# A hybrid decoder step: attention, retention, pages and sample states between the weight products of the input projection

## The chip, the cores and the metric

One core of a Trainium2 chip runs one inference step of a small hybrid decoder in a single launch. The metric is the device time of that launch in microseconds (us); smaller is better. The engines are TensorE (PE: matrix products, with PEld its weight loads), VectorE (DVE), ScalarE (ACT), GpSimd (POOL, which here only issues DMAs and clears a few tiles) and SyncE (SP, which here issues the DMAs of the weights).

## What is computed

264 tokens (256 of a prompt, and one token for each of 8 samples) go through two layers. The change touches the first mixer, which the reference states so (cut):

```python
proj = x @ w_in                       # 2048 -> 7168 + 2048 columns
qa, ka, va, qr, kr, vr, gr = split(proj)
ya = stick_breaking(qa, concat(past_k, ka), concat(past_v, va))   # 8 heads of 128
    # z = q k^T * scale + bias; log_fail = -softplus(z) where masked
    # w = exp(log_sigmoid(z) + suffix_sum(log_fail)); y = w v
qr, kr = rotary(qr), rotary(kr) * scale
yr, s_new = retention(qr, kr, vr, s0)                             # 8 heads, value width 256
    # s_new = gamma**n * s0 + k^T v (decayed); y = (q k^T * decay) v + q s0 (decayed)
yr = rms(yr) * silu(gr)
out = concat(ya, yr) @ w_out
```

For the prompt there is no past and the states start at zero. Each sample has 256 past positions in 2 pages of 128 (keys and values: 32 pages of 512 KB in all) and a retention state of 8 x 128 x 256 (half of it is 512 KB; 16 halves, each read, renewed and written back).

## The kernel before, in words

Activations lie feature-major: a tile of 128 features by 264 tokens (`T`) is a matmul's moving operand, and a weight block of 128 x 128 its stationary one. Each of the float32 weights is split into a high and a low part (`hi`, `lo`, in the format fp32r that the products use), as are the activations (`xh`, `xl`), and three matmuls (hi x xh, hi x xl, lo x xh) make one product. The weights come as chunks of 1 MB (128 x 2048): SP loads a chunk into one of the slots of `raw`, ScalarE writes `hi` (`split_hi`), VectorE writes `lo` over `raw` (`split_lo`), both two chunks ahead, and TensorE works through the chunk in four steps of 12 matmuls, one for each accumulator `acc0` to `acc3`. I call such a quarter of a chunk a step. Four chunks make a panel of 512 output columns, which ScalarE or VectorE then evicts.

The phases of weight products stand in a list (`plan`): ab (the input projection above, 72 chunks), out_ab (24), up0, down0, bc, dt, ssd (64), out_ssd, up1, down1. `products` has a hook, `side(j, n)`, which is called behind step n of chunk j and may issue other matmuls; ssd already runs its whole mixer that way: per group of 8 heads (8 groups) it issues 8 spreads (L2045), 8 state reads (L2055), 8 head products (L2076, L2077), a state product of 8 matmuls (L2084, L2085), transposes (L1786) and a few more, all between the products of 64 chunks.

The first mixer does not. Before, ab runs as a loop of 9 turns of two panels without a side. Then TensorE does stick-breaking attention, rotary turns and page scores in one block of code, page values and retention in a second, the samples' states in a third (`ret_outer`, `ret_read`), and the normalization of the heads in a fourth, before the first product of out_ab. There a page or a state is the stationary operand and one column the moving one:

```python
m = mm(aux[3][:, c:c + 1], pg[:, h, :], pt[:, QA + h, SEQ + b:SEQ + b + 1], ...)   # page_scores
```

Pages pass through 3 buffers (`page`), states through 5 (`s0buf`), loaded and stored by POOL in the order of its program, which also holds the waits for the buffers. All of these live in the space of `xh`, `xl` and `x`, which the projection no longer needs then. The gates (silu of `gr`) go to DRAM and back.

Of the kernel before, what the change touches and what calls it, by code (L numbers as in the profile page):

```python
# [7 lines left out]
F32 = mybir.dt.float32  # L8
# [7 lines left out]
P = 128  # L16
D = 2048
SEQ = 256
NB = 8
# [37 lines left out]
def raw_slot(j, body):  # L57

    return {1: (0,), 8: (0, 1, 2, 3, 0, 1, 4, 5)}.get(body, range(NRAW))[j] if body in (1, 8) else \
        (j + 1) % (NRAW - 1) if body == 64 else j % NRAW  # L60


def hi_slot(j, body, turn=0):

    return 0 if body == 1 else (j + 1) % (NHI - 1) if body == 64 else (j + turn) % NHI
# [32 lines left out]
def plan():  # L98
    phases = [
        Phase("ab", 9, 2, 4, False), Phase("out_ab", 2, 2, 6, True),  # L100
# [40 lines left out]
YT_AT, HS_AT, BT_AT, CB_AT, ST_AT, XT_AT, LAST_YT = 4, 8, 12, 20, 22, (24, 26), 24  # L141

# [60 lines left out]
def constants():  # L203
# [20 lines left out]
    by_sample = (j[:, None] < 64) & (j[:, None] % 32 == np.arange(NB)[None, :])  # L224
# [23 lines left out]
def param_layout():  # L248
    at = 0
    for name, width in (("lng", 4 * KT), ("lnb", 4 * KT), ("sbias", H), ("fcw", DEPTH * 3 * 2 * FT),  # L250
                        ("fcb", DEPTH * 2 * FT), ("scw", 4 * CT), ("scb", CT), ("dskip", XST),
                        ("normw", XST), ("dtb", 1), ("alog", 1)):
        PARAM[name] = (at, at + width)
        at += width
    return at
# [12 lines left out]
    "att_in", "consts_in", "conv_base", "conv_done", "conv_silu", "conv_tap",  # L268
    "decay_in", "ffn_out", "ffn_state_in", "ffn_sum", "ffn_tile",
    "gate_in", "gate_out", "kv_out", "ln_a", "ln_cen",  # L270
    "ln_delta", "ln_delta2", "ln_fin", "ln_mean", "ln_norm", "ln_qsum", "ln_sq", "ln_sqrt", "ln_sum", "ln_total", "ln_var", "page_in0", "page_in1",
    "page_in2", "page_used", "pages_in", "rn_a", "rn_b", "rn_bc", "rn_inv", "rn_sq", "rn_sqrt", "rn_sum",
    "rot_c", "rot_done", "rot_m", "rot_p", "rs_in0", "rs_in1", "rs_in2", "rs_in3", "rs_in4", "rs_km", "rs_new",
    "rs_o", "rs_out0", "rs_out1", "rs_out2", "rs_out3", "rs_out4", "rs_t", "rs_tc", "rs_y", "rs_yc", "rt_k",
    "rt_out", "rt_p", "rt_s", "rt_st", "rt_stc", "rt_t", "rt_v", "rt_y", "rt_yc", "sb_L",
    "sb_arg", "sb_cap", "sb_e", "sb_incl", "sb_lf", "sb_m", "sb_na", "sb_part", "sb_vs", "sb_vt", "sb_w",
    "sb_y", "sb_ycopy", "sbz", "sbz_s", "sconv_in", "sconv_out", "small_set",
    "ssd_sum", "x_back", "x_hi", "x_in", "x_lo", "x_out", "y_out",
    "dt_raw", "dt_a", "dt_c", "cum_out", "cd_out", "cd_in", "sel_in", "sel_r", "decay_in0", "decay_in1",
# [7 lines left out]
def build(nc, d):  # L287
# [8 lines left out]
    with ctx:  # L296

        NRB = 5
# [3 lines left out]
        with nc.sbuf_tensor("work", [P, 3 * KT * T], F32) as work:  # L302
            pass
        with nc.sbuf_tensor("workr", [P, 3 * KT * T], F32R) as workr:
            pass
# [11 lines left out]
        extra = sb("extra", [P, 3 * 512 + 384 + NB])  # L317
# [42 lines left out]
        banks = [aux, acc]  # L360


        at = 0
        upper, at = carve(work, at, P)
        rot, at = carve(work, at, P)
        mask, at = carve(work, at, 384)
        cap, at = carve(work, at, 384)
        trig, at = carve(work, at, 4, T)
        decay, at = carve(work, at, H, 384)
        tend, at = carve(work, at, H, 2)  # L370
        c0, c1 = CONST["upper"][0], CONST["tend"][1]
        assert at == c1 - c0, (at, c1 - c0)
        work_consts = work[:, 0:at]
        att0 = at
        temps = []
        for _ in range(2):
            zs, at = carve(work, at, 384)
            e_, at = carve(work, at, 384)
            lf, at = carve(work, at, 384)
            temps.append((zs, e_, lf))  # L380
        vtok = []
        ktw = []
        for _ in range(2):
            v, at = carve(work, at, 2, 256)
            vtok.append(v)
            v, at = carve(work, at, 2, P)
            ktw.append(v)
        NPB = 3
        pg0 = at
        page = []  # L390
        for _ in range(NPB):
            v, at = carve(work, at, H, P)
            page.append(v)

        ebuf = [temps[0][1], temps[1][1], carve(stage[:, :, :].rearrange("p a b -> p (a b)"), 0, 384)[0]]
        turned = []
        for _ in range(2):
            v, at = carve(work, at, T)
            turned.append(v)
        retp, _ = carve(pj, KA * T, H, 256)  # L400
        assert at <= 3 * KT * T, (at, 3 * KT * T)

        at = att0
        s0buf = []
        for _ in range(NRB):
            v, at = carve(work, at, H // 2, 256)
            s0buf.append(v)
        vts, at = carve(work, at, 2048)
        assert at <= 3 * KT * T
        kts, _ = carve(work, c1 - c0 - H * 2 - H * 384, 1024)  # L410
        ktm = [carve(work, c1 - c0 - H * 2 - H * 384 + 1024 * (1 + n), 1024)[0] for n in range(2)]

        silg = pt[:, KA:KA + 2 * H, :]
        rinv, at = carve(work, (KT + CK * LOOK) * T, T)
        rsq, at = carve(work, at, 2, 2, T)
        assert at <= 2 * KT * T, at
# [15 lines left out]
        raw_end, hi_end = raw[:, NRAW - 1, :], hi_plain[:, NHI - 1, :]  # L432
# [46 lines left out]
        def obank(h):  # L479

            return acc[h // 2][:, (h % 2) * 256:(h % 2) * 256 + 256]

# [18 lines left out]
        def load_chunk(eng, ph, i, j):  # L501
# [4 lines left out]
            if ph.name == "out_ssd" and i.reg is None and raw_slot(j, ph.body) == NRAW - 1:  # L506
                eng.wait_ge(used, ph.chunk0)
# [47 lines left out]
        def split_loop(eng, ph, split, src, evac, first=0, end=None, led=0, follow=None, mid=None, front=None):  # L555
# [26 lines left out]
            if front is not None:  # L582
                body(Step(0), False, front)
                with eng.Fori(0, stop - 1) as r:
                    body(Step(1, r), False)
# [70 lines left out]
        def _(pool):  # L656
# [7 lines left out]
            for n in range(4):  # L664
                pool.wait_ge(drained, 4 * (PHASES["ab"].panel0 + 14 + n) + 8)
                pool.dma_start(d["gate"][:, 4 * n:4 * n + 4, :], stage[:, :, :]).then_inc(R["gate_out"], 16)


            pool.wait_ge(used, PHASES["out_ab"].chunk0)
            pool.wait_ge(R["x_lo"], XB)  # L670
            c2 = CONST["decay"][0]
            pool.dma_start(work_consts[:, 0:c2 - c0], d["const"][:, c0:c2]).then_inc(R["att_in"], 16)
            pool.wait_ge(drained, 4 * PHASES["out_ab"].panel0 + 4)
            pool.wait_ge(R["pages_in"], 16)
            n = 0
            for cache in ("ck", "cv"):
                for b in range(NB):
                    for k in range(NPG):
                        v = pool.value_load(pages_sb[0:1, b * NPG + k:b * NPG + k + 1], min_val=0, max_val=NPHYS - 1)
                        if n >= NPB:  # L680
                            pool.wait_ge(R["page_used"], n - NPB + 1)
# [28 lines left out]
            for u in range(NRB - 1):  # L710
                ret_load(u)
# [1588 lines left out]
```

## Time and profile before

| | us |
|---|---|
| median of 3 runs | 3424.61 (3418.01 to 3427.3) |
| the profiled execution, own time | 3422.77 |
| its span, first to last instruction | 3421.1 |
| TensorE busy in the span | 3295.0 (96%) |
| VectorE busy | 1980.3 (58%) |
| ScalarE busy | 1638.3 (48%) |
| HBM traffic over the span | 175 GB/s |

TensorE is busy nearly throughout, so the share alone says little. Its clock has two levels, 1.2 and 2.4 GHz; the profile gives the granted mean of a stretch as a part of 2.4 GHz. In the answers by stretch the columns are: the stretch in us from the span's start, its length, the busy time (and number of instructions) of PE, PEld, DVE, ACT and POOL, the granted clock, the share of the 16 DMA engines, GB/s. A matmul on plain float32 shows as two instructions (x2 for one call), one on fp32r as one; "128\*64 128x256" means a stationary operand of 128 x 64 and a moving one of 128 x 256.

### The profile page before, as it was taken

Reading aid. Unit: us, or ns where it says so; the run is one execution under the profiler, and the core shown is the slowest. Engines: PE = TensorE matmul, PEld = TensorE weight load, DVE = VectorE, ACT = ScalarE, POOL = GpSimd, SP = SyncE. Lnnn points to the kernel's source line nnn. Section 1 sums busy time; section 2 is a strip of 40 time slices with the busy share of each in tenths; the row PEclk is TensorE's granted clock in tenths of the full one; section 3 lists DMA queues with packets and bytes.
Section 4 is the critical chain, followed back from the end, with each engine's and each line's share of the span. In section 5 each row is a group of like instructions: output and inputs, shape, how many; then the busy total and the mean of one; then the engine's idle time right before and its main releaser. Section 6 shows DMA issues by size and latency. Waiting matters only on the chain.

```text
span 3421.1 us, 60330 instructions
## 1 busy us (share of the span) xinstructions
PE 3295.0 (96%) x24851; PEld 3123.8 (91%) x24851; DVE 1980.3 (58%) x2487; ACT 1638.3 (48%) x1722; POOL 115.7 (3%) x206
## 2 busy tenths in 40 slices
PE   7999989989899999999899999999998999999997
PEld 7999988769899999999899777777998999999997
DVE  4333332246765565665766666666667565666666
ACT  3333333024554555544456555665645455455453
POOL 0000011100000000000000110110000000000000
PEclk9999968569999999999999999999999999999998
DMA  5444553525344544644455555554543544546452
GB/s 218 174 184 183 192 209 113 181 95 182 132 160 183 196 161 183 211 167 176 151 190 210 188 200 183 194 192 175 195 164 140 196 166 179 195 167 211 166 186 91
DMA packets 93949, 601.94 MB, mean 176 GB/s; under 512 B 10848, under 2 KB 10848, under 8 KB 32128
## 3 DMA queue, kind: packets, MB, share of 16 engines
q1 hardware_dynamic: 68256, 498.17, 38.9%
q0 software_dynamic: 25568, 102.01, 9.0%
q8 instruction: 89, 1.46, 0.2%
q14 instruction: 36, 0.29, 0.0%
HBM read 560.82 MB, written 39.32 MB: 175 GB/s over the span
## 4 chain that ended last, share of the span: by engine, by line
PE 91%; DVE 5%; issue 2%; ACT 1%; DMA 1%; POOL 0%; DVEq 0%; ACTq 0%; POOLq 0%; SPq 0%
PE acc L618 27%; PE acc L619 26%; PE acc L620 25%; PE aux L2055 2%; PE acc L1939 2%; PE aux L1952 2%; PE aux L1846 1%; PE aux L2076 1%; DVE lo L552 1%; PE acc L1857 1%; PE aux L2045 1%; DVE x L1492 1%; PE aux L1786 1%; DVE xl L1498 1%; PE acc L1798 0%
## 5 line engine op out<-in xcount | busy, mean ns | idle before, releaser
L618 PE MATMUL acc<-xh,hi 128*128 128x264 f32 x7552 | 2178.3, 288 | 73.2 <-DVE lo L552 38.0
L619 PE MATMUL acc<-xl,hi 128*128 128x264 f32 x7552 | 2152.8, 285 | 0.0
L620 PE MATMUL acc<-xh,lo 128*128 128x264 f32 x7552 | 2144.5, 284 | 0.0
L618 PEld LDWEIGHTS acc<-xh,hi 128*128 128x128 f32 x7552 | 1428.7, 189 | 122.8 <-issue 69.3
L552 DVE TENSOR_TENSOR lo<-raw,hi 128x2048 fp32r<-128x2048 f32 x473 | 1075.7, 2287 | 625.2 <-ACT hi L542 625.2
L619 PEld LDWEIGHTS acc<-xl,hi 128*128 128x128 f32 x7552 | 1429.4, 189 | 0.7
L620 PEld LDWEIGHTS acc<-xh,lo 128*128 128x128 f32 x7552 | 1426.4, 189 | 0.0
L542 ACT ACTIVATE hi<-raw 128x2048 fp32r<-128x2048 f32 x473 | 894.9, 1907 | 625.7 <-DMA raw<-in_w 370.8
L541 ACT ACTIVATE xh<-pj 128x1056 fp32r<-128x1056 f32 x144 | 156.0, 1084 | 363.6 <-PE acc L620 279.4
L549 DVE TENSOR_TENSOR xl<-pj,xh 128x1056 fp32r<-128x1056 f32 x144 | 180.6, 1254 | 242.7 <-ACT hi L542 239.6
L1310 DVE SCALAR_TENSOR_TENSOR stage<-acc,par,stage 128x255 f32<-128x255 f32 x352 | 168.6, 479 | 24.9 <-DVE stage L1310 24.4
L848 ACT ACTIVATE stage<-acc,par 128x264 f32<-128x264 f32 x176 | 100.4, 570 | 140.9 <-PE acc L620 140.9
L1641 DVE SCALAR_TENSOR_TENSOR x<-aux,pj,x 128x512 f32<-128x512 f32 x64 | 47.9, 748 | 62.5 <-PE aux L2045 62.5
L1443 DVE SCALAR_TENSOR_TENSOR work<-work,acc 128x256 f32<-128x256 f32 x64 | 24.1, 417 | 80.4 <-PE acc L1939 80.4
L2055 PE MATMUL aux<-x,raw 128*8 128x512 f32 x128 | 65.6, 594 | 0.0
L1952 PEld LDWEIGHTS aux<-pj,work 128*128 128x128 f32 x256 | 55.7, 330 | 9.8 <-issue 9.8
L1939 PE MATMUL acc<-work 8*128 8x256 f32 x128 | 60.0, 647 | 3.9 <-DVE work L1432 3.9
L953 ACT ACTIVATE work<-pj 128x528 f32<-128x528 f32 x8 | 5.0, 641 | 120.9 <-DVE pj L1447 116.3
L1952 PE MATMUL aux<-pj,work 128*128 128x1 f32 x256 | 57.0, 353 | 0.0
L1527 DVE TENSOR_TENSOR pj<-stage 128x528 f32 (+1 forms) x44 | 31.2, 708 | 40.5 <-ACT stage L1022 40.5
L1939 PEld LDWEIGHTS acc<-work 8*128 8x128 f32 x128 | 39.9, 325 | 13.7 <-issue 4.2
L1649 DVE SCALAR_TENSOR_TENSOR pj<-pj,par,aux 128x256 f32<-128x256 f32 x32 | 15.3, 480 | 57.9 <-PE aux L2077 57.9
(300 smaller groups left out, 1858.7 us busy)
## 6 DMA issues: line engine op xcount, KB each, us to landing
raw<-in_w SPq DMA_DIRECT2D x473, 1024.0 KB, 4.8
x<-in_ssm POOLq DMA_DIRECT2D x32, 512.0 KB, 3.9
out_ssms<-x POOLq DMA_DIRECT2D x32, 512.0 KB, 3.6
work<-in_ck POOLq DMA_DIRECT2D x16, 512.0 KB, 3.8
work<-in_cv POOLq DMA_DIRECT2D x16, 512.0 KB, 3.8
work<-in_ret POOLq DMA_DIRECT2D x16, 512.0 KB, 4.8
out_rets<-work POOLq DMA_DIRECT2D x16, 512.0 KB, 5.3
pj<-cumd POOLq DMA_DIRECT2D x32, 256.0 KB, 4.2
```

The costliest lines, as they stand in the source:

```text
L541: act.activation(xh[:, CK * s:CK * s + CK, :], src[:, CK * kc:CK * kc + CK, :], ACT.Copy)
L542: act.activation(hi[:, ph.hi(j), :], raw[:, r, :], ACT.Copy).then_inc(hi_done, 1)
L549: dve.tensor_tensor(xl[:, CK * s:CK * s + CK, :], src[:, CK * kc:CK * kc + CK, :], xh[:, CK * s:CK * s + CK, :].bitcast(F32), ALU.subtract)
L552: dve.tensor_tensor(lo[:, r, :], raw[:, r, :], hi[:, ph.hi(j), :].bitcast(F32), ALU.subtract).then_inc(lo_done, 1)
L618: pe.matmul(out, hi[:, s, w], xh[:, a, :], start=kc == 0 and k == 0, stop=False)
L619: pe.matmul(out, hi[:, s, w], xl[:, a, :], start=False, stop=False)
L620: m = pe.matmul(out, lo[:, r, w], xh[:, a, :], start=False, stop=kc == ph.kc - 1 and k == CK - 1)
L848: a(dst(q, n), acc[n][:, 0:T], ACT.Identity, bias=col(bias), scale=col(w))\
L1310: ins = stt(y[:, k:SEQ], h[:, 0:SEQ - k], one(w[:, width - 1 - k, :], n), y[:, k:SEQ], ALU.mult, ALU.add)
L1939: m = mm(obank(h), ktm[b % 2][0:NB, h * P:h * P + P], vts[0:NB, h * 256:h * 256 + 256], start=True, stop=True)
L1952: m = mm(aux[2][:, c:c + 1], s0buf[u % NRB][:, k, e * P:e * P + P], pt[:, QR + h, SEQ + b:SEQ + b + 1], start=True, stop=True)
L2055: mm(bank_ys[0:NB, :], cz[:, NB * b:NB * b + NB], hbuf[u % 3][:, (b % 2) * 512:(b % 2) * 512 + 512], start=b == 0, stop=b == NB - 1).then_ ...
```

## The change

ab becomes one turn of 18 panels, unrolled, with `ab_side` as its side: every matmul of the mixer is issued behind a fixed step s = 4 j + n of the 288 steps. The panels' order changes so that what the mixer needs comes first (a table: `AB_PANELS`, queries and keys of retention first, gates last), and tables of numbers say at which step each piece stands. Pages and states become the moving operand: the stationary one is a block of 128 x 32 in which one column is the query (`zq`, `qd`) or the weight (`wz`) of a head and the others are zero, so that the 8 (or 4) heads accumulate in rows 32 b to 32 b + 31 of one bank. The outer products for the states take stacked high and low parts in fp32r (`kstk`, `vstk`, 72 rows) in place of 8 rows of float32. All of it shares four banks: `outer`, `reads`, `att`, `heads`; `att` is passed from use to use by two counters (`att_full`, `att_free`). The buffers: ab now uses 5 of 6 `raw` slots and 3 of 4 `hi` slots, and the mixer works in the others, in `x_` and in `extra`; states and pages share one ring of 3 slots of 512 KB (before 5 and 3). The norm's square root and reciprocal become Ln and Exp on ScalarE; the gates no longer pass through DRAM; the samples' sticks are summed by a scan on VectorE.

```diff
-        Phase("ab", 9, 2, 4, False), Phase("out_ab", 2, 2, 6, True),
+        Phase("ab", 1, 18, 4, False), Phase("out_ab", 2, 2, 6, True),
...
+AB_PANELS = [("qr", 0), ("kr", 0), ("vr", 0), ("vr", 1), ("qr", 1), ("kr", 1), ("vr", 2), ("vr", 3), ("qa", 0),
...
+RET_AT = [56 + 16 * h for h in range(H)]
+UNIT_AT = [(78, 142)[u // NB] + 5 * (u % NB) for u in range(2 * NB)]
+SB_AT = [200 + 9 * h for h in range(H)]
+KPAGE_AT = [190 + 2 * n for n in range(NB * NPG)]
+VPAGE_AT = [240 + 2 * n for n in range(NB * NPG)]
+RET_OUT, SB_OUT, PAGE_TURN, PAGE_BACK = 13, 11, 234, 275
...
+            for n in range(3):
+                ring_load(n)
...
+                pool.wait_ge(R["rs_new"], 4 * (n + 1))
+                pool.dma_start(ret_half(d["rets"], n), unit[n % 3]).then_inc(R[f"ring_out{n % 3}"], 16)
...
+            for n in range(units + 2, units + 2 * NB * NPG):
+                ring_load(n)
+                if n == units + NB * NPG + 4:
+                    pool.wait_ge(drained, 4 * AB_PANELS.index(("va", 1)) + 8)
+                    pool.dma_start(d["kv"], pt[:, KA:KA + 2 * H, :]).then_inc(R["kv_out"], 16)
...
-            products(pe, PHASES["ab"], 0)
...
+            def outer_of(u, x):
+
+                pe.wait_ge(R["rs_km"], u + 1)
+                pe.wait_ge(R["att_free"], ATT["vs", 2 * (u // NB) + x] + 1)
+                if u or x:
+                    pe.wait_ge(R["rs_new"], 4 * u + 2 * x)
+                for k in range(2 * x, 2 * x + 2):
+                    m = mm(outer[:, (k % 2) * 256:(k % 2) * 256 + 256], ktm[u % 2][0:72, k * P:k * P + P],
+                           vstk[0:72, k * 256:k * 256 + 256], start=True, stop=True)
+                m.then_inc(R["ob_full"], 1)
+
+            def read_unit(u, x):
+
+                b = u % NB
+                pe.wait_ge(R["qd_set"], u + 1)
+                pe.wait_ge(R["rs_new"], 4 * u + 2 * x + 2)
...
+                for k in range(2 * x, 2 * x + 2):
+                    m = mm(reads[32 * (b % 4):32 * (b % 4) + 32, o:o + 256], qd[u % 2][:, k, :], unit[u % 3][:, k, :],
+                           start=k == 0, stop=k == 3)
...
+            def page_scores(n, x):
 
                 b, k = n // NPG, n % NPG
                 pg = page_at(n)
...
+                for h in range(4 * x, 4 * x + 4):
+                    m = mm(reads[32 * (b % 4):32 * (b % 4) + 32, o:o + P], zq[b % 2][:, h, :], pg[:, h, :],
+                           start=h == 0, stop=h == H - 1)
...
+            products(pe, PHASES["ab"], 0, ab_side)
```

Three places in the order of the program. First TensorE in the attention and the page scores. Before (aux and acc are the PSUM banks, pj the projected tiles, work the buffers), outside of any product:

```order
L1805 MATMUL acc<-pj 128x256
L1806 MATMUL acc<-pj 128x128
L1798 MATMUL acc<-pj,work 128x264
L1846 MATMUL aux<-pj,work 128x1 x8
L1786 MATMUL aux<-cons,pj 128x128 x2
L1822 MATMUL aux<-work 128x384
L1823 MATMUL aux<-work,cons 128x128
L1846 MATMUL aux<-pj,work 128x1 x8
```

Now, at steps 200 and 201 (L625 to L627 are the weight products, x holds the page):

```order
L627 MATMUL acc<-xh,lo 128x264
L2143 MATMUL aux<-pj 128x256
L2144 MATMUL aux<-pj 128x128
L2185 MATMUL aux<-x 32x128 x4
L625 MATMUL acc<-xh,hi 128x264
L626 MATMUL acc<-xl,hi 128x264
L627 MATMUL acc<-xh,lo 128x264
```

The page scores of one page were 8 matmuls of one moving column; they are now two calls of four matmuls of 128 moving columns, behind two consecutive steps, and a head's scores (L2143, L2144) stand in front of one of them.

Second TensorE in the samples' states. Before, 16 units in a row (L1939 the outer products, L1952 the reads of 4 heads with 2 halves each):

```order
L1939 MATMUL acc<-work 128x256 x8
L1952 MATMUL aux<-pj,work 128x1 x8
L1939 MATMUL acc<-work 128x256 x4
L1952 MATMUL aux<-pj,work 128x1 x8
L1939 MATMUL acc<-work 128x256 x4
L1952 MATMUL aux<-pj,work 128x1 x8
```

Now (lo is the stacked values, raw the weights and values of a retention head, L2080 and L2081 that head's output), behind one step and the next but one behind it:

```order
L627 MATMUL acc<-xh,lo 128x264
L2107 MATMUL aux<-lo,hi 128x256 x2
L2080 MATMUL aux<-raw 128x256
L2081 MATMUL aux<-raw 128x128
L2080 MATMUL aux<-raw 128x256
L2081 MATMUL aux<-raw 128x128
L625 MATMUL acc<-xh,hi 128x264
```

A unit's 4 outer products are cut in two calls two steps apart, its reads in two more three and five steps behind the first, and the prompt's retention shares steps with them.

Third ScalarE in steps 236 to 239 (L909 evicts the gates with silu, L548 is the split of a chunk, L991, L998 and L1000 work for an attention head):

```order
L909 ACT_TABLE_LOAD
L909 ACTIVATE stage<-acc 128x264
L548 ACTIVATE hi<-raw 128x2048
L991 ACTIVATE raw<-aux,par 128x384
L909 ACTIVATE stage<-acc 128x264
L998 ACT_TABLE_LOAD
L998 ACTIVATE raw<-raw 128x384
L1000 ACT_TABLE_LOAD
L1000 ACTIVATE raw<-raw,small 128x384
L909 ACT_TABLE_LOAD
L909 ACTIVATE stage<-acc 128x264 x2
```

Before, the same head's work on ScalarE (L893, L895) had no split and no eviction between:

```order
L880 ACTIVATE work<-acc,par 128x384
L893 ACT_TABLE_LOAD
L893 ACTIVATE work<-work 128x384
L895 ACT_TABLE_LOAD
L895 ACTIVATE work<-work,small 128x384
```

The splits that feed the next chunks now stand in one queue with the head's exponentials, the evictions and their table loads.

## Rows read from the trace of the kernel before

**Rows 1.** The span by stages: length, busy time by engine, clock, DMA.

```profile
19.00:440.00 421.00, 421.00 (x3454) 421.00 (x3455) 160.76 (x71) 159.93 (x142) 1.60 (x3) 1.00 0.48 187
440.00:754.00 314.00, 287.39 (x1296) 244.04 (x1294) 96.56 (x197) 77.92 (x123) 37.46 (x71) 0.64 0.44 145
754.00:908.00 154.00, 146.32 (x1173) 144.76 (x1172) 108.75 (x99) 74.58 (x59) 0.54 (x1) 0.98 0.44 156
...
1815.00:2407.00 592.00, 585.57 (x3848) 466.94 (x3847) 390.26 (x589) 346.34 (x475) 57.89 (x108) 1.00 0.55 190
```

**Rows 2.** TensorE in order of time: first and last product of ab, first of out_ab.

```profile
18.80 0.59 PE L618 MATMUL acc<-xh,hi 128*128 128x264 f32 x1 [18.80 <-DVE lo L552]
...
440.13 0.28 PE L620 MATMUL acc<-xh,lo 128*128 128x264 f32 x1
...
754.21 0.59 PE L618 MATMUL acc<-xh,hi 128*128 128x264 f32 x1
```

**Rows 3.** The separate stage, 440 to 754: costliest TensorE groups by form.

```profile
L1939 PE MATMUL acc<-work 8*128 8x256 f32 x128 | 60.0, 647 | 3.9 <-DVE work L1432 3.9
L1952 PE MATMUL aux<-pj,work 128*128 128x1 f32 x256 | 57.0, 353 | 0.0
L1846 PE MATMUL aux<-pj,work 128*128 128x1 f32 x256 | 44.1, 303 | 0.0
```

**Rows 4.** A stretch of it, in the samples' states, columns as in rows 1.

```profile
625.00:725.00 100.00, 100.00 (x340) 83.30 (x339) 23.75 (x60) 0.00 (x0) 12.68 (x24) 0.50 0.43 135
```

**Rows 5.** Steps of ssd, TensorE alone: start, length, line, operation.

```profile
1996.01 0.60 PE L1786 MATMUL aux<-cons,pj 128*128 128x128 f32 x4
...
1996.36 0.37 PE L618 MATMUL acc<-xh,hi 128*128 128x264 f32 x1
...
2019.06 0.28 PE L620 MATMUL acc<-xh,lo 128*128 128x264 f32 x1
2019.27 0.65 PE L2076 MATMUL aux<-raw,x 128*64 128x256 f32 x2
...
2020.07 0.39 PE L618 MATMUL acc<-xh,hi 128*128 128x264 f32 x1
...
2021.53 0.28 PE L620 MATMUL acc<-xh,lo 128*128 128x264 f32 x1
2021.74 0.50 PE L2045 MATMUL aux<-hi,selr 40*128 40x512 f32 x1
2022.17 0.39 PE L618 MATMUL acc<-xh,hi 128*128 128x264 f32 x1
...
2023.60 0.28 PE L620 MATMUL acc<-xh,lo 128*128 128x264 f32 x1
2023.81 1.02 PE L2055 MATMUL aux<-x,raw 128*8 128x512 f32 x2
2024.76 0.49 PE L2084 MATMUL aux<-hi_plain 128*128 128x128 f32 x2
...
2026.57 0.36 PE L618 MATMUL acc<-xh,hi 128*128 128x264 f32 x1
```

**Rows 6.** What TensorE waited for in ssd: total us, times, longest.

```profile
PE aux L2076 <- DVE raw L1624: 3.2, 4, 0.9
```

**Rows 7.** DMA issues of the separate stage: size, median us to landing.

```profile
work<-in_ck POOLq DMA_DIRECT2D x16, 512.0 KB, 3.8
out_kv<-pj POOLq DMA_DIRECT2D x1, 2112.0 KB, 15.7
```

**Rows 8.** Groups of ScalarE and VectorE in ssd: busy us, mean ns of one.

```profile
L542 ACT ACTIVATE hi<-raw 128x2048 fp32r<-128x2048 f32 x65 | 124.0, 1911 | 97.8 <-PE acc L620 97.8
L1129 ACT ACT_TABLE_LOAD x17 | 21.8, 1283 | 0.3
...
L552 DVE TENSOR_TENSOR lo<-raw,hi 128x2048 fp32r<-128x2048 f32 x64 | 146.0, 2282 | 10.9 <-ACT hi L542 10.9
```

More of the change, by code:

```diff
@@ L373, in build @@
[L373 to L416, printed above, removed]
+        raw_end, hi_end = raw[:, NRAW - 1, :], hi_plain[:, NHI - 1, :]
+        raw_endr, hi_endr = lo[:, NRAW - 1, :], hi[:, NHI - 1, :]
@@ new lines, in build @@
+        outer, reads, att, heads = aux
+        ring = [carve(x_, 1024 * n, 1024)[0] for n in range(3)]
+        unit = [v.rearrange("p (h e) -> p h e", h=4) for v in ring]
+        page = [v.rearrange("p (h e) -> p h e", h=H) for v in ring]
+        trig, at = carve(x_, 3072, 4, T)
+        assert at <= KT * T
+        ysr, wz, zq = x_[:, 3072:3584], [], []
+        at = 3072
+        for buffers in (wz, zq):
+            for _ in range(2):
+                v, at = carve(x_, at, H, 32)
+                buffers.append(v)
@@ L661, in _ @@
             pool.dma_start(sel, d["const"][:, CONST["sel"][0]:CONST["sel"][1]]).then_inc(R["sel_in"], 16)
[L664 to L669, printed above, removed]
+            pool.memset(vstk[0:96, :].bitcast(F32), 0.0).then_inc(R["stk_zero"], 1)
+            pool.memset(kstk[0:96, :].bitcast(F32), 0.0).then_inc(R["stk_zero"], 1)
@@ new lines, in gate_tile, with ret_keys @@
+            def gate_tile(p, n, i):
+                wait_acc(act, ab, Step(0), p, n)
+                if i:
+                    act.wait_ge(R["gr_gated"], i)
+                else:
+                    act.wait_ge(R["att_full"], ATT["rn", H - 1] + 1)
+                a(stage[:, n, :], acc[n][:, 0:T], ACT.Silu).then_inc(drained, 1)
+            def ret_keys(h):
+                att_ready("kt", h)
+                act.wait_ge(R["att_in"], 32)
+                if h:
+                    act.wait_ge(R["att_full"], ATT["st", h - 1] + 1)
+                for c in range(2):
+                    ins = a(ktw[:, c, :], att[:, c * P:c * P + P], ACT.Identity, scale=tend[:, h, c:c + 1])
+                ins.then_inc(R["att_free"], 1)
@@ new lines, in ret_out @@
+            def ret_out(h):
+                pe.wait_ge(R["att_free"], ATT["rs", h] + 1)
+                pe.wait_ge(R["hb_free"], h)
+                for u in range(2):
+                    o = u * 256
+                    mm(heads[:, o:o + 256], vtok_r[:, 0, u * P:u * P + P], gp[:, 0:SEQ], start=True, stop=False)
+                    m = mm(heads[:, o + P:o + 256], vtok_r[:, 1, u * P:u * P + P], gp[:, 256:384],
+                           start=False, stop=True)
+                m.then_inc(R["hb_full"], 1)
@@ new lines, in read_turn, with ret_sum @@
+            def read_turn(f):
+                att_turn("rt", f)
+                pe.wait_ge(R["ysr_in"], f + 1)
+                for k in range(4):
+                    m = turn(att[:, k * P:k * P + P], ysr[:, k * P:k * P + P])
+                m.then_inc(R["att_full"], 1)
+            def ret_sum(h):
+                att_turn("rn", h)
+                pe.wait_ge(R["rn_half"], h + 1)
+                mm(att[:, 0:T], ones, stage[:, 2 * (h % 2), :], start=True, stop=True).then_inc(R["att_full"], 1)
```

1034 lines of the change are left out of this document (613 added, 421 removed).

## The prediction

> **What bounds the kernel now.** I read the span by stages first, because the 96% of TensorE is a mean over unlike stages. In ab TensorE is busy without a gap at clock 1.00, and in ssd for 585.6 of 592 us, also at 1.00 [rows 1]: there the number of its instructions sets the time, and VectorE (390 us) and ScalarE (346 us) fit beside it. Between the two stands the stage that the change dissolves: from the end of ab's last product (440.1 + 0.3) to out_ab's first (754.2) pass 313.8 us [rows 2], with TensorE busy for 287 of them but at a mean clock of 0.64 [rows 1]. In the samples' states, 625 to 725, it is 0.50, the lower of the two levels, with TensorE busy all the time [rows 4]; before it stood 421 us of dense products at 1.00, and out_ab's return to 0.98. So the stage is bound by TensorE at half its clock in dependent small matmuls: outer products (60.0 us), reads of the states (57.0) and page scores (44.1) are its largest groups [rows 3]. No weight product runs in it.
>
> **What goes.** The 313.8 us go whole; every matmul of theirs comes back in another form, between products. Out_ab's first microseconds at the lower clock go too: 154 us at 0.98 [rows 1] is some 3 us that a warm start saves.
>
> **What comes, at which price.** The nearest thing in the trace is ssd, which already issues a mixer behind its steps. Its steps give the prices [rows 5]; the pitch of products is 0.12 us (264 columns; ab: 421.6 us, 72 chunks of 48 matmuls), so a call costs the distance from the last L620 to the next L618 less 0.12.
>
> - 512 columns of plain float32 (L2055): 2024.76 - 2023.60 - 0.12 = 1.04 us.
> - Eight such matmuls of 128 columns behind it: 2026.57 - 2024.76 = 1.81, or 0.226 each. So of the 1.04, 0.90 are columns and 0.14 the entry.
> - 384 columns in two matmuls (L2076, L2077): 2020.07 - 2019.06 - 0.12 = 0.89.
> - 512 columns of fp32r (L2045): 2022.17 - 2021.53 - 0.12 = 0.52.
> - Four transposes (L1786): 1996.36 - 1996.01 = 0.35.
>
> Now the calls of the changed ab. State reads are 32 calls of 2 x 256 columns and pages 64 calls of 4 x 128, all plain float32: 96 x 1.04 = 99.8 us. Outer products: 32 calls of 2 x 256 fp32r columns, 16.6. Retention scores, attention scores and attention outputs: 24 x 0.89 = 21.4. Retention states and stick sums: 16 x 1.04 = 16.6. Retention outputs, 768 columns, 2 x 0.89 less one entry: 8 x 1.65 = 13.2. Rotary and norm sums, 24 of 264 columns at 2.06 x 0.226 + 0.14 = 0.60: 14.4. 102 transposes: 8.9. Sum 190.9.
>
> The same price list on ssd itself gives 64 x (0.52 + 1.04 + 0.89) + 8 x 1.81 + 8 x 0.89 + 8 x 0.60 + 151 x 0.0875 = 196.4 us. It really paid 592 - 64 x 5.856 = 217.2 [rows 1], its waits of 6.4 included. I therefore scale by 1.106: 211 us. Bounds: 191 (list alone) and 240 (a quarter over it).
>
> The turned operand does not itself pay: the reads took 57.0 us at 0.50 [rows 3, 4], which at 1.00 would be no less than 28.5, and now cost 32 x 1.04 = 33. What pays is the clock of the neighbours and that chains of dependent steps are filled with products. On the one-column form the Trainium skill (TensorEngine Tiling (Array Packing), Instruction Overhead) says that a moving operand of one column costs as much as one of about 60; the trace shows more than that, 57.0 us for 256 instructions, 0.22 us each at the lower clock [rows 3, 4].
>
> **What may wait.** TensorE's side steps wait in order for VectorE and ScalarE, which also make the splits. Their load is no bound: ab's and the stage's work together is 257 and 238 us [rows 1] of some 640, less than the two thirds and three fifths of ssd. But chains are short of slack in places. In steps 222 to 239 no page call lengthens the steps; ScalarE owes four splits (1.91) and some eight table loads (1.28) [rows 8], 18 of about 31 us, beside the exponentials of an attention head and of the pages. A late exponential there holds the head's sum on TensorE, and the bank `att` behind it. ssd, with the same mixture, lost 3.2 us in 4 waits at its worst place [rows 6]. Bounds: nothing, and 40 us (a dozen places late by a split and a table load, 3.2 us each); I take 8, near ssd.
>
> POOL's queue: states pass a ring of 3 slots with 15 steps (over 30 us) between uses of a slot, against a store and a load of about 5 us each. Pages leave a slot 4 to 5 steps, over 10 us, and land in 3.8 [rows 7]. The longest item put in front of them is the store of keys and values (15.7 us when it shared the queues with other loads) behind value page 4; page 5 follows it in the queue and is wanted some 19 us later. That is covered, with little to spare: 15.7 + 3.8 = 19.5. If the cover fails it is a few us once. ab's and the stage's traffic over the new length is (187 x 421 + 145 x 314) / 641 = 194 GB/s, ssd's 190. SP's queue holds the weights alone; 5 slots served ssd too. The gates' trip through DRAM, POOL's clears and the start's small loads lie beside the first chunks; I cost them at nothing, and at 1 us if the first split comes late.
>
> **Sum.** ab begins at 18.8 and takes 421.6 + 211.1 + 8 = 640.7, so out_ab begins at 659.5 in place of 754.2: 94.7 us, and 3.1 for its clock, 97.8 in all. The profiled execution has 3422.8 of its own, so 3325; it lies 1.8 under the median of the runs, so **3327**.
>
> **The rivals.**
> 1. *Cheaper.* No waits and the bare list: 20 + 8 us less, 3299. Against it: ssd paid 1.106 times the list.
> 2. *Dearer by waits.* The places above add up to their bound, or the entry into 32-column operands costs more: 3350 to 3395. One form of it is a drain. The heads of ssd, stationary 64 columns, cost 0.89 where 0.68 are columns: an entry of 0.21 against 0.14, so 96 calls by 0.07 are 7 us. If instead each of the 96 calls paid twice the largest entry seen (L2045: 0.52 less 0.23 at the pitch of products, 0.29), it would be 56 us: 3383. The Trainium skill (TensorEngine Tiling (Array Packing), Key Properties) has the rule behind this one: a change of tiling mode drains TensorE. By that rule every page call would pay on entry and return; the 0.21 of the heads shows little of it.
> 3. *Slower than before: the clock.* TensorE was busy without a gap at 0.50 from 625 to 725 [rows 4]. If the small matmuls pull the clock down in the page and state steps (64 and some 80 steps of about 2.5 us), these 360 us double: 3690. It decides from 98 us of work at half clock, about 40 such steps. Against it: ssd spends 217 of 592 us in the same kind of call and holds 1.00. The Trainium skill (TensorE: Matmul & The Clock Gate, What's actually happening) has the half rate as default, which activity lifts; rows 1 show both levels.
> 4. *Nothing gained.* The work costs between products what it cost alone, 287 us at the old clock, and 25 more of waits: 3422. Only the clock's remaining low would do it.
>
> **Chances.** Forecast (3305 to 3350) 0.62; rival 1 0.10; rival 2 0.22; rival 3 0.04; rival 4 0.02. The range 3295 to 3368 takes in rival 1's value and half of rival 2, and leaves out less than 2 in 10. Faster by over 0.3% (10 us, about what a measurement of this kernel tells from no change) 0.94, within it 0.02, slower 0.04.
>
> **What would show it.** Right: one stretch from 18.8 to about 660 at clock near 1.00, TensorE busy for all but 10 to 15 us; page steps 1.0 to 1.1 us longer than bare ones; out_ab at 1.00 from its first product. Wrong: a clock of 0.50 in page or state steps; waits of TensorE for ScalarE's exponentials around steps 222 to 240 or for page loads over 3 us each; calls with 32-column operands well over 1.1 us.

## The result: 3290 us, below the range

The changed kernel takes 3290.09 us (median of 4 runs, 3289.05 to 3291.66) against 3421.36 for the kernel before beside it (4 runs): a ratio of 0.9615, 95% interval 0.9598 to 0.9632. Forecast were 3327 and 3295 to 3368. It is faster, as forecast; the gain is 131 us where 97.8 were expected. The profiled execution took 3290.35, 132.4 less than the one of before with its 3422.77.

The span by stages (length, busy time by engine, clock, DMA), which answers to [rows 1]; line numbers are those of the changed kernel, where L625 to L627 are the weight products:

```profile
19.00:624.00 605.00, 605.00 (x4534) 551.39 (x4535) 263.40 (x335) 276.70 (x319) 42.27 (x79) 1.00 0.55 196
624.00:777.00 153.00, 144.66 (x1174) 143.31 (x1172) 111.92 (x101) 76.03 (x61) 0.53 (x1) 0.98 0.50 170
1683.00:2274.00 591.00, 584.57 (x3851) 466.13 (x3850) 390.54 (x589) 346.67 (x475) 57.91 (x108) 1.00 0.55 190
```

The separate stage with its mean clock of 0.64 is gone. ab, now with all the mixer's calls in it, is one stretch at 1.00 in which TensorE is never idle; out_ab and ssd are as long as before to within some 1 us. Where ab begins and ends (TensorE in order of time, answers to [rows 2]; the second line is out_ab's first product), and all that TensorE waited for from 18 to 625 (total us, times, longest):

```profile
18.91 0.59 PE L625 MATMUL acc<-xh,hi 128*128 128x264 f32 x1 [18.91 <-DVE lo L558]
...
624.03 0.28 PE L625 MATMUL acc<-xh,hi 128*128 128x264 f32 x1
```

```profile
PE acc L625 <- DVE lo L558: 18.9, 1, 18.9
```

The only wait is that of the start, before the first product. So ab takes 605.1 us where 640.7 were forecast: 421.6 for the products as before, and 183.5 for the calls where 219.1 stood (the list of 190.9, 20.2 for its scale, 8 of waits). The 35.6 us between are nearly all of the error, and the question is which calls are cheaper than the list.

Calls that stand alone in their step, from the same timeline (start, length, line, stationary*, moving operand):

```profile
67.73 0.28 PE L627 MATMUL acc<-xh,lo 128*128 128x264 f32 x1
67.86 0.60 PE L2039 MATMUL aux<-pj,raw 128*128 128x264 f32 x2
68.11 0.48 PE L625 MATMUL acc<-xh,hi 128*128 128x264 f32 x1
...
120.09 0.28 PE L627 MATMUL acc<-xh,lo 128*128 128x264 f32 x1
120.21 0.59 PE L2065 MATMUL aux<-pj 128*128 128x256 f32 x2
120.64 0.39 PE L2066 MATMUL aux<-pj 128*128 128x128 f32 x2
120.78 0.37 PE L625 MATMUL acc<-xh,hi 128*128 128x264 f32 x1
120.99 0.28 PE L626 MATMUL acc<-xl,hi 128*128 128x264 f32 x1
...
145.25 0.28 PE L627 MATMUL acc<-xh,lo 128*128 128x264 f32 x1
145.37 0.40 PE L2107 MATMUL aux<-lo,hi 72*128 72x256 f32 x2
145.61 0.29 PE L625 MATMUL acc<-xh,hi 128*128 128x264 f32 x1
...
393.89 0.28 PE L627 MATMUL acc<-xh,lo 128*128 128x264 f32 x1
394.10 1.06 PE L2185 MATMUL aux<-x 128*32 128x128 f32 x8
395.09 0.39 PE L625 MATMUL acc<-xh,hi 128*128 128x264 f32 x1
395.32 0.28 PE L626 MATMUL acc<-xl,hi 128*128 128x264 f32 x1
```

A call's price is read as in the forecast: from the start of the product before it to that of the product behind it, less 0.12. The 264 columns of a rotary call cost 68.11 - 67.73 - 0.12 = 0.26 (list 0.60), 384 columns of retention scores 0.57 (list 0.89), an outer product 0.24 (0.52); a page call costs 395.09 - 393.89 - 0.12 = 1.08 (1.04). A part of what a call takes falls behind it and is not in this price: the distance of the next two products is 0.23 after the page call and 0.21 after the scores, not 0.12. The same reading over ab gives for calls that stand alone (the counts take in those that share a step):

| call | count | list | measured | behind it |
|---|---|---|---|---|
| page, 4 x 128 columns, stationary 128x32 | 64 | 1.04 | 1.08 | 0.11 |
| state read, 2 x 256, stationary 128x32 | 32 | 1.04 | 1.07 | 0.11 |
| scores and outputs, 384 columns | 24 | 0.89 | 0.57 | 0.08 |
| retention state; stick sum (512 columns) | 8; 8 | 1.04 | 0.67; 0.78 | 0.19; 0.09 |
| retention output, 768 columns | 8 | 1.65 | 1.23 | 0.09 |
| rotary, norm sum, 264 columns | 24 | 0.60 | 0.25 | 0.19 |
| outer product, rounded float32, 72 rows | 32 | 0.52 | 0.24 | 0.00 |
| four transposes | 17 | 0.35 | 0.35 | 0.08 |

Added up over the 171 steps that hold a call, the prices make 165.6 us and what falls behind them 17.9. The list had the calls right whose operand has 32 columns, and the transposes. All others, whose operands are full or 72 rows high, were priced 0.26 to 0.42 too high. A row for them stood in the trace before: ssd's score call (L2099, L2100), alone in its step there (TensorE of the kernel before):

```profile
1855.77 0.28 PE L620 MATMUL acc<-xh,lo 128*128 128x264 f32 x1
1855.89 0.59 PE L2099 MATMUL aux<-pj 128*128 128x256 f32 x2
1856.32 0.39 PE L2100 MATMUL aux<-pj 128*128 128x128 f32 x2
1856.46 0.37 PE L618 MATMUL acc<-xh,hi 128*128 128x264 f32 x1
```

That is 0.57 us for 384 columns, where [rows 5] give 0.89 for the 384 of a head with 64 stationary columns.

### The profile page after: what moved, and what is told of

Read it like the earlier page. It is cut to its first block, busy times and chain, and to the rows that moved or that the text cites. A ratio compares the mean times of both kernels' runs of the same rounds, so it can differ in the third digit from the quotient of the medians.

```text
span 3288.5 us, 59783 instructions
## 1 busy us (share of the span) xinstructions
PE 3188.0 (97%) x24637; PEld 3007.0 (91%) x24637; DVE 1989.8 (61%) x2557; ACT 1679.0 (51%) x1778; POOL 125.1 (4%) x222
## 4 chain that ended last, share of the span: by engine, by line
PE 93%; DVE 5%; ACT 1%; issue 1%; DMA 1%; DVEq 0%; POOL 0%; ACTq 0%; POOLq 0%; SPq 0%
PE acc L625 28%; PE acc L626 27%; PE acc L627 27%; PE aux L2348 2%; PE aux L2369 1%; DVE lo L558 1%; PE aux L2199 1%; PE aux L2185 1%; PE aux L2120 1%; PE aux L2022 1%; PE aux L2338 1%; DVE x L1728 1%; DVE xl L1734 1%; PE aux L2370 0%; DVE x L1718 0%
## 5 line engine op out<-in xcount | busy, mean ns | idle before, releaser
L625 PE MATMUL acc<-xh,hi 128*128 128x264 f32 x7552 | 2194.4, 291 | 74.3 <-DVE lo L558 38.6
L627 PE MATMUL acc<-xh,lo 128*128 128x264 f32 x7552 | 2143.5, 284 | 0.0
L625 PEld LDWEIGHTS acc<-xh,hi 128*128 128x128 f32 x7552 | 1427.6, 189 | 141.0 <-issue 85.1
L627 PEld LDWEIGHTS acc<-xh,lo 128*128 128x128 f32 x7552 | 1425.2, 189 | 0.0
L548 ACT ACTIVATE hi<-raw 128x2048 fp32r<-128x2048 f32 x473 | 896.7, 1907 | 544.4 <-PE acc L627 317.9
L900 ACT ACTIVATE pj<-acc 128x264 f32<-128x264 f32 x56 | 21.7, 390 | 92.5 <-PE acc L627 92.5
L1539 DVE SCALAR_TENSOR_TENSOR x<-x,aux 128x256 f32<-128x256 f32 x64 | 24.1, 418 | 65.2 <-PE aux L2107 65.2
L1850 DVE SCALAR_TENSOR_TENSOR pj<-stage,par,pj 128x255 f32<-128x255 f32 (+2 forms) x96 | 46.1, 481 | 2.3
L879 ACT ACTIVATE small<-small 128x1 f32<-128x1 f32 x48 | 9.7, 203 | 73.1 <-DVE stage L1443 58.7
L2369 PE MATMUL aux<-raw,x 128*64 128x256 f32 x128 | 41.2, 404 | 3.2 <-DVE raw L1860 3.2
L1868 DVE TENSOR_TENSOR x<-x,extra 128x512 f32<-128x512 f32 x64 | 43.7, 682 | 0.0
```

The lines of the kernel that those rows point to most:

```text
L548: act.activation(hi[:, ph.hi(j), :], raw[:, r, :], ACT.Copy).then_inc(hi_done, 1)
L625: pe.matmul(out, hi[:, s, w], xh[:, a, :], start=kc == 0 and k == 0, stop=False)
L627: m = pe.matmul(out, lo[:, r, w], xh[:, a, :], start=False, stop=kc == ph.kc - 1 and k == CK - 1)
L2369: mm(y[:, 0:SEQ], xdt[:, 0, o:o + HD], w[:, 0:SEQ], start=True, stop=False)
```

## The experiments

Two theories of the difference. **A**: a stationary operand of 64 columns or fewer makes each moving column cost double. **B**: a call pays a fixed price at its border with the products, whatever its operand; from the second set of runs on its heir **P**: only a call with a narrow operand pays it. All kernels are edits of the changed kernel; where a range stands with a time, it is the median of 4 runs.

**Wide operands for pages and state reads.** The query columns lie 128 apart in a buffer of zeros, and each matmul takes a window of 128 columns that holds one of them, at its output row:

```diff
-mm(reads[32 * (b % 4):32 * (b % 4) + 32, o:o + P], zq[b % 2][:, h, :], pg[:, h, :], ...)
+c = P - 1 + P * h - 32 * (b % 4) - h
+mm(reads[:, o:o + P], zq[b % 2][:, c:c + P], pg[:, h, :], ...)
```

Page values and state reads likewise. The buffers of zeros, now larger, move into tiles of `pj` and are cleared at other steps.

> Changes the stationary operand of the page calls and of the state reads from 128x32 to 128x128 (the same query columns, one of them not zero in each matmul, read through a window that slides over a buffer of zeros); every product stays the same, so the output does too. Theory A, a float32 matmul whose stationary operand has 64 columns or fewer costs twice as much for each moving column as one with 128, and one with 128 has a floor of about 0.113 us an instruction: a page call of 4x128 columns falls from 1.08 us in the changed kernel's trace to 0.90, a state read of 2x256 from 1.07 to 0.46 to 0.57, so 64 x 0.18 + 32 x 0.5 to 0.6 = 27 to 31 us less than the changed kernel's 3290, 3259 to 3263. Theory B, a call of such products pays a fixed price for entering and leaving the stream of weight products, whatever its stationary operand: no change, 3285 to 3295. Theory C, a wider stationary operand takes longer to load and the load is not hidden: a page call rises by up to 8 x 0.08, some 3300 to 3330.

Measured: 3263.01 us (3260.86 to 3264.16), ratio to before 0.9537 (0.9521 to 0.9553), 27 less than the changed kernel. A page call:

```profile
376.85 0.28 PE L623 MATMUL acc<-xh,lo 128*128 128x264 f32 x1
376.97 1.05 PE L2177 MATMUL aux<-x,pj 128*128 128x128 f32 x8
377.77 0.37 PE L621 MATMUL acc<-xh,hi 128*128 128x264 f32 x1
```

It costs 0.80 in place of 1.08 and begins 0.12 after the last product, not 0.21. As many columns move, and more weights are loaded. A state read costs 0.67, with 0.19 behind it, in place of 1.07 and 0.11. With what falls behind, each of these 96 calls takes some 0.3 less, 29 us in all; a new wait of 1.0 us takes some of it back. So theory B's fixed price for any call is ruled out, and theory C's dearer load. Theory A forecast the total; P would too.

**The old operands, moved.** The page, or half a sample's state, is stationary again and one column moves (page values and state reads likewise):

```diff
-mm(reads[32 * (b % 4):32 * (b % 4) + 32, o:o + P], zq[b % 2][:, h, :], pg[:, h, :], ...)
+mm(reads[:, o + 8 * (b % 4) + h:o + 8 * (b % 4) + h + 1], pg[:, h, :], zq[b % 2][:, h, h:h + 1], ...)
```

> Keeps the move and undoes the turning of the operand: the page (128x128) or half a sample's state (128x128) is the stationary operand again and one column of query moves; 4 matmuls for a page call as before, 4 in place of 2 for a state read. The columns land across partitions and are read as rows, so the pages' and the samples' part of the output is not the reference's; all later work is done on them as before. Theory A: each matmul costs the floor of two instructions, 2 x 0.113, so a page call 0.90 in place of 1.08 and a state read 0.90 in place of 1.07, 64 x 0.18 + 32 x 0.17 = 17 us less, about 3273: the turning bought nothing, all of the gain is the move. The theory that turning the operand is itself part of the gain: the page and state calls cost clearly more than with it, 3300 to 3350.

Measured: 3266.93 us (3265.71 to 3267.3), 23 less than the changed kernel.

```profile
380.20 0.28 PE L627 MATMUL acc<-xh,lo 128*128 128x264 f32 x1
380.32 0.94 PE L2189 MATMUL aux<-x 128*128 128x1 f32 x8
381.13 0.37 PE L625 MATMUL acc<-xh,hi 128*128 128x264 f32 x1
```

0.81 a page call: one moving column costs what 128 do with a full operand. The turned operand, as the change made it, costs 23 us, so the gain comes from the other parts of the change. The move is one of them, but no run undoes the rest alone: the outer products, for one, were busy for 60.0 us in the separate stage [rows 3], most of them at clock 0.50 [rows 4], and now cost 32 x 0.24 = 7.7 us, and how much of that is their new format and how much the move is not shown.

**One matmul of four left in each page call.** The loops over four heads become `for h in (7 * x,):`.

> Leaves three of the four matmuls out of each page call (one head of four is computed, so the pages' part of the output is not the reference's). Theory A: the call falls with its columns, from 1.08 us to 0.27, so 64 x 0.81 = 52 us less, about 3238. Theory B (a fixed price for entry and exit, the columns at the 0.11 us of a matmul of two instructions with a full stationary operand's rate): the call falls to 0.6 or more, at most 30 us less, 3260 or above.

Measured: 3252.2 us (one run), between the two forecasts, with 3.9 us of waits (for a norm and for a value page) that the changed kernel does not have.

```profile
385.10 0.28 PE L627 MATMUL acc<-xh,lo 128*128 128x264 f32 x1
385.31 0.41 PE L2185 MATMUL aux<-x 128*32 128x128 f32 x2
385.65 0.39 PE L625 MATMUL acc<-xh,hi 128*128 128x264 f32 x1
```

One matmul costs 0.43 and four 1.08: 0.22 for each, and 0.21 that does not go away with the columns (0.32 with what falls behind the call, against full operands at 0.65 / 384 = 1.7 ns a column). Theory A, which has 0.27 here, is wrong, and so is theory B's 0.6 or more. From here on theory P: 1.7 ns for each plain float32 column, and some 0.32 for a call with a narrow operand.

**The page scores in one block**, which undoes the move for them:

```diff
-KPAGE_AT = [190 + 2 * n for n in range(NB * NPG)]
+KPAGE_AT = [220] * (NB * NPG)
...
-                        if s == KPAGE_AT[k] + x:
+                        if s == KPAGE_AT[k]:
```

> Undoes the move of one part: all 32 score calls of the pages stand in one block behind step 220 in place of one call a step in 190 to 221; the operand stays turned and all other calls stay. Theory that what the move takes away is the waiting for data, and with it the fallen clock: a page of two calls takes 2.16 us, and three page buffers whose load lands 3.8 us after its issue come round in about 6.3 us, so TensorE waits little for each page and the block costs 0 to 10 us if the clock holds at 1.00, 3290 to 3300; if the waits bring the clock to 0.50 the 34.6 us of the block double, 3320 to 3330. The theory that calls cost by where they stand between weight products (0.1 us behind each): the block is 3 us cheaper, 3287.

Measured: 3301.5 us (one run), 11 more. TensorE's new waits (L2185 is the page scores, L2136 the norm sum), and the stretch of the block (columns as in the stage rows above):

```profile
PE aux L2185 <- DMA x<-in_ck: 9.0, 12, 2.0
PE aux L2136 <- DVE stage L1557: 4.7, 3, 3.4
```

```profile
443.60:484.00 40.40, 31.43 (x258) 27.34 (x257) 4.83 (x10) 4.50 (x5) 7.91 (x15) 0.96 0.65 205
```

Without products between them the pages wait for their loads. The clock is at the lower level for a part of the block only: 0.96 in mean, 0.83 from 450 to 460, and not 0.50 throughout.

**Both halves of a page in one step**, narrow as in the changed kernel: `KPAGE_AT[k] + x` and `VPAGE_AT[k] + x` lose their `+ x`.

> Issues both halves of a page (8 matmuls in place of two times 4) behind the same step, every second step, as narrow (128x32) calls as in the changed kernel; nothing else changes. Theory P, formed on the runs before this one: a plain float32 call pays 1.67 ns for each moving column and, where its stationary operand is narrower than 128 columns, a price of its own of about 0.32 us for the entry and the exit, once a call: 32 prices fewer, 32 x 0.32 = 10 us less than the changed kernel, 3279 to 3281. Theory A, the price of a narrow operand is paid for each column (twice that of a wide one): as many columns as before, so at most the 0.1 us behind a call is saved, 0 to 3 us, 3287 to 3291.

Measured: 3281.67 us (3280.91 to 3281.94); 8.4 less, near P's 10 and far from A's 0 to 3.

```profile
384.69 0.28 PE L627 MATMUL acc<-xh,lo 128*128 128x264 f32 x1
384.91 1.94 PE L2185 MATMUL aux<-x 128*32 128x128 f32 x16
386.77 0.39 PE L625 MATMUL acc<-xh,hi 128*128 128x264 f32 x1
```

Eight matmuls cost 1.96 in one call and 2 x 1.08 in two. Now the same edit on the kernel with wide operands:

> The kernel with wide page and state operands, with both halves of a page behind one step. Theory P: a wide call pays for its columns alone (0.81 us and 0.08 behind it for 512 columns, which is the 0.85 of 512 columns at 1.67 ns and little more), so there is no price to save: 0 to 2 us less than 3263, 3260 to 3263. The theory that every call pays for leaving and entering the weight products, wide or not: 8 to 10 us less, 3253 to 3255.

Measured: 3260.62 us (one run) against 3263.01, as P has it. The difference is no larger than the spread of the runs there (3260.86 to 3264.16), but the calls tell it plainly: eight matmuls cost 1.70 in one call with 0.08 behind it, and 2 x 0.81 with 2 x 0.08 behind them in two (medians of the calls that stand alone). Wide calls have no price to save.

**The reverse: 384 columns made narrow.** Scores and attention outputs keep their columns and take 64 of 128 stationary ones:

```diff
-mm(att[:, 0:256], k[:, 0:P], q[:, 0:SEQ], start=True, stop=True)
-mm(att[:, 256:384], k[:, P:SEQ], q[:, P:SEQ], start=True, stop=True)
+mm(att[0:64, 0:256], k[:, 0:64], q[:, 0:SEQ], start=True, stop=True)
+mm(att[0:64, 256:384], k[:, P:P + 64], q[:, P:SEQ], start=True, stop=True)
```

> The reverse: 24 calls with 384 moving columns (scores of attention and retention, attention's output) keep their columns and lose half of their stationary operand, 64 columns in place of 128, so half of these scores and outputs is not computed and what is read there is left from earlier. Theory P: the calls that stand alone (11, or behind a wide call) rise from 0.57 us to about 0.89, the price that the forecast had taken for all of them; those that share a step with a narrow page call, 13, pay nothing more or little: 3 to 8 us more, 3293 to 3298. Theory A: 384 columns twice as dear, +0.64 for each of 24, 15 us more, 3305.

Measured: 3297.16 us (one run), 7 more.

```profile
120.10 0.28 PE L627 MATMUL acc<-xh,lo 128*128 128x264 f32 x1
120.32 0.65 PE L2065 MATMUL aux<-pj 128*64 128x256 f32 x2
120.80 0.38 PE L2066 MATMUL aux<-pj 128*64 128x128 f32 x2
121.11 0.39 PE L625 MATMUL acc<-xh,hi 128*128 128x264 f32 x1
```

121.11 - 120.10 - 0.12 = 0.89: half the result, at the very price that the list had for all such calls. In company with a 32-column page call the sum of both rose from 1.74 to 1.87, so a part is paid there too.

**96 columns**: the wide kernel's page windows cut to `c:c + 96`.

> The kernel with wide operands, but the page calls with 96 columns of stationary operand in place of 128 (the samples' rows lie 24 apart, so the pages' part of the output is read from the wrong rows). It asks where the price of narrow operands begins. If with anything under 128: the page call rises from 0.81 to about 1.08 us, 64 x 0.3 = 19 us more than 3263, 3282. If only with 64 and fewer: no change, 3260 to 3264.

Measured: 3263.32 us (one run), a page call by the same reading 0.79. At 96 columns there is no price yet; where between 64 and 96 it begins, no run shows.

**The same in ssd**, on top of the wide pages and states. A head takes the columns of its pair, a state read a window of 128 of which 8 count:

```diff
-mm(bank_ys[0:NB, :], cz[:, NB * b:NB * b + NB], hbuf...)
+mm(bank_ys[:, :], cz[:, NB * b:NB * b + P], hbuf...)
...
-mm(y[:, 0:SEQ], xdt[:, 0, o:o + HD], w[:, 0:SEQ], start=True, stop=False)
+mm(y[:, 0:SEQ], xdt[:, 0, o:o + P], w[:, 0:SEQ], start=True, stop=False)
```

> The kernel with wide page and state operands, and in ssd too the stationary operands widened to 128 columns: the 64 head products take the columns of a pair of heads (each head's result lies in its half of the partitions, in 256 columns of its own, and two VectorE operations of 64 partitions take the place of one), the 64 state reads a window of 128 columns of which 8 are used. The output is the same. Theories P and A: 0.32 us or a little more saved for each of 128 calls, 41 us of the 590 of ssd, 3220 to 3225 in place of the 3263 of the kernel with wide page and state operands alone, if no other engine becomes the bound there (VectorE was busy 390 of 592 us in the kernel before and gets 32 operations more). The theory that the gain in the first stage came from something else than the width, for instance from the buffers' other place or the fewer memsets: no change, 3260 to 3266.

Measured: 3227.73 us (3226.98 to 3228.25), ratio 0.9438 (0.9422 to 0.9454). That is 35 us less, where 41 were expected. ssd falls by 34 us for 128 calls, 0.27 each, and stays bound by TensorE:

```profile
1654.00:2211.00 557.00, 550.62 (x3847) 483.79 (x3847) 407.62 (x621) 345.59 (x475) 57.91 (x108) 1.00 0.58 202
```

The rest is where a state read shares its step with a spread, an operand of 40 rows, as 23 do: such a step falls from 1.47 to 1.37 us only.

**And in rows**: on top of that, ssd's spreads contract over 128 rows, those added being zero.

```diff
-mm(bank_spread[:, :], selr[0:40, b:b + 1].to_broadcast([40, P]), xdr[0:40, :],
+mm(bank_spread[:, :], selr[:, b:b + 1].to_broadcast([P, P]), xdr[:, :],
```

> On top of the kernel with wide operands in pages, states and ssd: the 64 spreads of ssd (rounded float32, one matmul of 512 columns) contract over all 128 rows in place of 40; the rows added are zero on one side, so the output stays. A spread alone costs 0.52 us and 0.11 behind it, while the outer products of the first stage, also rounded float32, 72 rows and 2x256 columns, cost 0.24 in all. Theory P widened, an operand that fills only a part of the array's rows pays a price at the border too: 64 x 0.37 = 24 us less than 3228, 3203 to 3209. Theory that the price belongs to operands narrow in columns alone, and the spread's is of another kind: no change, 3225 to 3230.

Measured: 3207.37 us (3206.72 to 3207.79), ratio 0.9365 (0.9349 to 0.938): the fastest here. A spread, first with 40 rows (the kernel before this step), then with 128:

```profile
1706.84 0.28 PE L623 MATMUL acc<-xh,lo 128*128 128x264 f32 x1
1707.05 0.50 PE L2335 MATMUL aux<-hi,selr 40*128 40x512 f32 x1
1707.48 0.39 PE L621 MATMUL acc<-xh,hi 128*128 128x264 f32 x1
```

```profile
1708.13 0.28 PE L623 MATMUL acc<-xh,lo 128*128 128x264 f32 x1
1708.25 0.39 PE L2335 MATMUL aux<-hi,selr 128*128 128x512 f32 x1
1708.48 0.28 PE L621 MATMUL acc<-xh,hi 128*128 128x264 f32 x1
```

0.52 falls to 0.23, over three times the rows, and the 0.11 behind it goes too (the next two products stand 0.12 apart). The kernel is 20 us faster, where 24 were expected.

**Shorter chains in attention**, on the changed kernel: a head's value turn and sum stand `(0, 2, 3)` steps behind its scores in place of `(0, 3, 6)`, and `SB_OUT`, the distance of its output, is 6 in place of 11.

> Attention's chain at shorter distances: the sum stands 3 steps behind the scores in place of 6 (the value turn 2 in place of 3), the output 3 steps behind the sum in place of 5. In the changed kernel's trace the mask product, which the sum needs, ends 2.8 us (head 3) to 11.0 us (head 0) before the sum begins, and the weights, which the output needs, 4.1 to 7.7 us before it. Theory that there are no waits only because the distances in steps are longer than the chains: at half the distance waits come back, 1 to 3 us in the heads whose steps are short (3 and 4), 3 to 15 us in all, 3293 to 3305. Theory that other engines would in any case hold back no more than they do: no waits, 3290.

Measured: 3306.14 us (one run), 16 more, just over the bound. The waits that came, 10.5 us of it, and the stretch of the two longest (L2158 is the sum, L2167 the output):

```profile
PE aux L2158 <- ACT raw L1007: 8.2, 3, 3.9
PE aux L2167 <- ACT raw L1012: 2.3, 2, 1.5
```

```profile
490.00:530.00 40.00, 32.62 (x226) 30.18 (x224) 15.14 (x17) 23.40 (x29) 0.53 (x1) 0.91 0.30 105
```

Both are ScalarE's, the value copy that stands behind exponentials and the exponential itself. The clock accounts for up to 3.6 of the other 5 us: after waits of 3.9 and 3.5 us in this stretch TensorE worked for a time at the lower level, and the mean is 0.91 over 40 us. So these two waits cost more than their own length.

## Why the prediction missed its range

- **What goes: right.** 313.8 us went whole. TensorE holds 1.00 through ab.
- **The list of prices: the step that failed**, 25 of the 35.6 us. "512 columns of plain float32 (L2055)", "384 columns in two matmuls (L2076, L2077)" and "512 columns of fp32r (L2045)" are rows of operands with 8 and 64 columns and with 40 rows. They were taken for what columns cost, and applied to 104 calls whose operands are full, or 72 rows of 128 columns: 24 x 0.32 + 8 x 0.37 + 8 x 0.26 + 8 x 0.42 + 24 x 0.35 + 32 x 0.28 = 33.5 us too much (not all of it is saved: at 264 columns 0.19 of the 0.35 falls behind the call). The pages and reads stood 3.5 too low, and calls that share a step give back 5: an outer product and a read cost 1.41, alone 0.24 and 1.07, because what falls behind the one then lies inside the step. The split of 1.04 into "0.90 are columns and 0.14 the entry" read up to the next matmul alone: with the 0.11 behind it such a call takes 1.15 to 1.18, and the wide state read, 512 columns too, 0.67 + 0.19 = 0.86; the border has some 0.3. The forecast even had this price in hand, as the 0.29 of L2045 under its rival 2, and still gave the outer products the whole 0.52.
- **The scale of 1.106: right in size by luck, wrong in meaning.** It was to cover what the list missed. What it held was the part of a call's price that falls on the products behind it, 17.9 us here for the 20.2 taken; ssd has 20.6 behind its 197 steps, all of the excess over the list there. The excess also held ssd's 6.4 us of waits, so that waits were counted in the scale and once more in the 8; in ssd the list was too high by nearly as much, with 0.32 for each of 8 score calls and 0.35 for each of 8 of 264 columns.
- **Waits: 0 for the 8 taken**, at the lower bound, and the second part of the 35.6 us. The chains had more slack than the forecast read from step numbers; with half the distance waits came, at ScalarE, where the forecast looked for them. The value pages did not wait either: the store of keys and values landed in 9.1 us, not 15.7.
- **Out_ab's clock: the sign right, the size too large.** Out_ab now begins at 1.00, as forecast, and is 1.2 us shorter, not 3.1. The forecast put the whole of 154 x 0.02 at the start. The first ten us there lacked 0.16 x 10 = 1.6 us; the rest lies at the end, where TensorE waits for the next phase, 8.2 us before and 8.5 now, at 0.72 (900 to 909) and 0.71 (768 to 777), so that the mean stays 0.98. The start of out_ab before, then its start and its end in the changed kernel:

```profile
754.00:764.00 10.00, 10.00 (x70) 9.80 (x70) 7.15 (x7) 7.93 (x6) 0.00 (x0) 0.84 0.13 36
```

```profile
624.00:634.00 10.00, 10.00 (x85) 10.00 (x84) 9.99 (x8) 8.75 (x7) 0.00 (x0) 1.00 0.85 311
768.00:777.00 9.00, 0.74 (x4) 0.29 (x2) 8.24 (x14) 3.95 (x7) 0.00 (x0) 0.71 0.24 81
```

- **"The turned operand does not itself pay": right**, and stronger: undone it saves 23 us.
- **Rivals.** The clock held, so rival 3 is out (the lower level itself stands in [rows 4]; [rows 1] show 1.00 and means), and the block kept 0.96 in mean even with waits. Rival 1 ("no waits and the bare list", 3299, given 0.10) was nearest and still too dear. Rival 2's mechanism is real: the narrow calls pay at entry and return. The forecast priced it as an addition to 96 calls; it was in the list already, for those and for the calls that do not pay it. The Trainium skill (TensorEngine Tiling (Array Packing), Key Properties) says that a change of tiling mode drains TensorE; the runs agree in kind, with some 0.3 us for entry and return at 8, 32 and 64 columns, some 0.4 at 40 rows, and nothing to be seen at 96 columns or 72 rows. That the price is this drain is not shown: the runs show which operands pay it, not what the engine does then. The forecast weighed this rule against the 0.21 of the heads, which has it inside.

## What to carry to other kernels

When prices are read from a trace for another call, match the shape of the stationary operand in columns and rows before the count of moving columns; a row of the full shape is worth searching for even if it stands only once. Between full-width products, an operand with unused columns or rows of zeros can be cheaper than a small one: here 64 pages, 32 reads, 128 calls of ssd and 64 spreads together gave 83 us. Of a change with several parts, time the parts: here the turning lost 23 us of what the others earned, and the total alone did not tell.

## What the hardware showed that was not expected

- A call whose stationary operand has 8, 32 or 64 columns costs about 0.3 us more among full products than the same moving columns with 96 or 128, once a call, not for each matmul or column (0.43 us for one matmul, 1.08 for four, 1.96 for eight). One of 40 rows costs about 0.4 more than one of 128 (0.52 and 0.11 behind it, against 0.23), and 72 rows show no such price (0.24 for as many columns).
- Transposes are an exception that the runs don't explain. Four with 8 columns cost 132.56 - 132.09 - 0.12 = 0.35, no more than four with 128 [rows 5]. The Trainium skill (TensorEngine Tiling (Array Packing), Restrictions and Gotchas) has transpose mode excluded by column tiling, which would fit; no run here tests it.

```profile
132.09 0.28 PE L627 MATMUL acc<-xh,lo 128*128 128x264 f32 x1
132.20 0.60 PE L2022 MATMUL aux<-cons,pj 128*8 128x128 f32 x4
132.56 0.37 PE L625 MATMUL acc<-xh,hi 128*128 128x264 f32 x1
```

- Plain float32 with a full operand costs 1.7 ns for each moving column at clock 1.00 (384 columns 0.65 with what falls behind, 768 columns 1.32), but with one column no less than 0.2 a matmul (0.81 for four).
